# Column strips for the sums over time in a long-convolution filter

## The reference

```python
def hyena_filters(L, w1, b1, w2, b2, w3):
    ...
    h = (h @ w3.astype(f32)).reshape(L, 2, D_A)
    deltas = jnp.abs(jnp.linspace(MIN_DECAY, MAX_DECAY, D_A, dtype=f32))
    h = h * jnp.exp(-t * deltas)[:, None, :]
    h = h / jnp.sum(jnp.abs(h), axis=(0, 1), keepdims=True)
    return h[:, 0], h[:, 1]
```

## Time and profile before

| | us |
|---|---|
| median of three runs | 1622.42 (1619.22 to 1625.27) |
| the profiled execution | 1621.05 |
| its span, first to last instruction | 1619.3 |
| TensorE busy | 1511.1 (93%) |
| DVE busy | 691.1 (43%) |
| ACT busy | 466.4 (29%) |
| POOL busy | 91.9 (6%) |

### The profile page before, as it was taken

One profiled execution on the slowest core, in us unless ns is written; L12 is line 12 of the kernel. 1 busy time (PEld: TensorE's weight loads), 2 busy tenths in 40 slices (PEclk: granted clock), 3 DMA queues, 4 the chain that ended last, 5 costly groups with the idle time before them and its releaser, 6 DMA issues.

```text
span 1619.3 us, 20451 instructions
## 1 busy us (share of the span) xinstructions
PE 1511.1 (93%) x8098; PEld 1230.7 (76%) x8098; DVE 691.1 (43%) x1136; ACT 466.4 (29%) x770; POOL 91.9 (6%) x112
## 2 busy tenths in 40 slices
PE   4788999999899989999899998989999999999897
PEld 1587999999724434388788887878888999999786
DVE  4522223233232352477666776665432222223644
ACT  3332112121121110244444444454541111111321
POOL 2301000000032110100000000000000000000000
PEclk8788999999999999999999999999999999999999
DMA  9310233323300104300000000012220100110611
GB/s 372 141 53 30 79 109 105 120 105 120 141 27 26 62 26 169 118 6 6 20 5 15 5 5 15 0 61 74 79 108 29 40 30 28 35 33 16 231 53 52
DMA packets 29821, 111.16 MB, mean 69 GB/s; under 512 B 3371, under 2 KB 7599, under 8 KB 26064
## 3 DMA queue, kind: packets, MB, share of 16 engines
q1 hardware_dynamic: 28048, 103.46, 17.7%
q10 hardware_dynamic: 1728, 7.08, 1.1%
HBM read 93.86 MB, written 16.66 MB: 68 GB/s over the span
## 4 chain that ended last, share of the span: by engine, by line
PE 85%; DVE 7%; DMA 3%; ACT 2%; issue 2%; SPq 0%; POOL 0%; DVEq 0%; PEld 0%; POOLq 0%; ACTq 0%; PEldq 0%
PE bank L478 58%; PE bank L856 12%; PE bank L778 3%; PE bank L679 3%; PE bank L923 2%; PE bank L771 1%; DMA H<-w_mod_in 1%; PE bank L489 1%; DVE amax L1501 1%; PE bank L628 1%; PE bank L636 1%; DVE SCR L1508 1%; DMA H<-w_oo_in 1%; ACT KV L963 1%; PE bank L501 1%
## 5 line engine op out<-in xcount | busy, mean ns | idle before, releaser
L478 PE MATMUL bank<-H_r,WR_r 128*128 128x384 f32 x1728 | 352.8, 336 | 1.6 <-DVE H_r L1613 1.2
L478 PEld LDWEIGHTS bank<-H_r,WR_r 128*128 128x128 f32 x1728 | 302.6, 188 | 6.3 <-issue 4.2
L478 PE MATMUL bank<-H_r,SCR_r 128*128 128x384 f32 x480 | 161.0, 336 | 0.0
L478 PE MATMUL bank<-SCR 128*128 128x128 f32 x1168 | 141.3, 275 | 2.3 <-DVE H L1514 2.3
L478 PEld LDWEIGHTS bank<-SCR 128*128 128x128 f32 x1168 | 135.7, 192 | 3.2 <-issue 3.2
L478 PE MATMUL bank<-KV,WR 128*128 128x512 f32 (+3 forms) x352 | 126.5, 509 | 1.6 <-ACT KV L1142 1.3
L1181 ACT ACTIVATE SCR<-bank,nmax 128x1152 f32<-128x1152 f32 (+1 forms) x72 | 81.1, 1127 | 148.1 <-DVE nmax L1502 148.1
L478 PEld LDWEIGHTS bank<-KV,WR 128*128 128x128 f32 (+1 forms) x352 | 57.3, 171 | 62.7 <-issue 52.5
L856 PE MATMUL bank<-H_r,WR_r 128*128 128x512 f32 x432 | 99.8, 394 | 3.8 <-DVE SCR L1646 3.8
L478 PE MATMUL bank<-H_r,WX_r 128*128 128x384 f32 x384 | 99.4, 340 | 3.3 <-PEq L571 3.3
L856 PEld LDWEIGHTS bank<-H_r,WR_r 128*128 128x128 f32 x432 | 82.2, 190 | 21.3 <-DVE SCR L1646 4.0
(11 more groups left out here) (249 smaller groups left out, 2194.8 us busy)
## 6 DMA issues: line engine op xcount, KB each, us to landing
H<-w_mod_in SPq DMA_DIRECT2D x6, 2048.0 KB, 16.7
WR<-w_mod_in SPq DMA_DIRECT2D x12, 1024.0 KB, 7.0
SCR<-w_in_in SPq DMA_DIRECT2D x20, 512.0 KB, 3.4
SCR<-x_sample_in SPq DMA_DIRECT2D x16, 512.0 KB, 12.0
WR<-w_io_in SPq DMA_DIRECT2D x16, 512.0 KB, 3.4
sp_rows<-SCR SPq DMA_DIRECT2D x9, 512.0 KB, 2.6
KV<-sp_rows SPq DMA_DIRECT2D x9, 512.0 KB, 8.1
WR<-tf_in SPq DMA_DIRECT2D x4, 1024.0 KB, 4.9
```

Source lines behind the costliest of these rows:

```text
L478: last = nc.tensor.matmul(out, l, r, start=(n == 0), stop=(n == len(pairs) - 1))
```

## The change

The magnitudes of a tile (2 directions x 512 channels) are summed in four strips of 32 columns of the array, each with 32 columns of ones as weights and 256 channels of one direction as columns: strip 0 and 1 the two halves of the forward direction, 2 and 3 those of the backward one. The sums then stand on all 128 partitions (32 equal rows a strip), 256 columns in bank 6 and 256 in bank 7. ACT copies both to all partitions of `norm_rows`. In place of the transposes there are eight products with a selector column, which has a one in the first row of the two strips that belong together, and so adds the directions. POOL makes this selector at the start. The rest is the same.

```diff
-        sel = sb("sel", 2)
+        sel, sel_half = sb("sel", 2), sb("sel_half", 2)
...
-        norm_rows = WX[0:1, 0:2 * DA]
+        norm_rows = WX[:, 0:DA]
...
             def magnitude_sums(t):
                 pe.wait_ge(fh_mag, t + 1)
-                for j in range(2):
-                    last = nc.tensor.matmul(bank[0:1, 6 + t // PROMPT, :], ones[:, 0:1], f_mag[t % 2][:, j, :],
-                                            start=(t in (0, PROMPT) and j == 0), stop=(t >= PROMPT - 1 and j == 1))
+                for g in range(4):
+                    last = nc.tensor.matmul(bank[32 * g:32 * (g + 1), 6 + t // PROMPT, 0:256], ones[:, 0:32], f_mag[t % 2][:, g // 2, g % 2 * 256:(g % 2 + 1) * 256],
+                                            start=t in (0, PROMPT), stop=t >= PROMPT - 1)
                 last.then_inc(nrm_mm, 1)
...
                     for n in range(2 * CA):
-                        last = nc.tensor.transpose(bank[:, 7, n:n + 1], norm_rows[:, n * P:(n + 1) * P], ident[0:1, 0:1])
+                        last = nc.tensor.matmul(bank[:, 7, n:n + 1], norm_rows[:, (n // CA * 2 + n % 2) * P:(n // CA * 2 + n % 2 + 1) * P], sel_half[:, n % CA // 2:n % CA // 2 + 1], start=True, stop=True)
                     last.then_inc(nrm_T, 1)
...
-            nc.scalar.copy(split(norm_rows, 2), bank[0:1, 6:8, :]).then_inc(nrm_cp, 1)
+            nc.scalar.copy(split(norm_rows, 2), bank[:, 6:8, 0:256]).then_inc(nrm_cp, 1)
...
+            link(nc.gpsimd.tensor_tensor(sel_half[:, :], ident[:, 0:64:32], ident[:, 64:P:32], ALU.add))
             link(nc.gpsimd.tensor_tensor(sel[:, :], ident[:, 0:2], ident[:, 32:34], ALU.add))
```

## The result

The changed kernel takes 1631.83 us in the median (1628.24 to 1634.54), the kernel before beside it 1624.62 (1619.22 to 1626.56): a ratio of 1.0048, 95% interval 1.0034 to 1.0062. Forecast were 1616.1 us and faster; it became slower, by 7.8 us of 1624, and lies outside the range. By its number it is rival E, to which the prediction gave 3%, within 1.5 us (1630.5). One slow execution further down, of 5284.1 us among the seven with filter products over all 128 rows, is left out of that run's ratio.

A forecast was written before the change was run, and what follows sets the result against it. TensorE alone was taken to set the filter stage's pace. DVE's product of tile 8 starting 8.7 us earlier, +1.1 for the selector and +1.3 for the tail's clock gave -6.3 us: 1616.1 us from 1622.42, range 1611.5 to 1620.5.

The forecast's parts named there:

- rival E: TensorE's clock falls in the middle of the filter stage: 4.7 us a turn, +8 us, 1630.5 us; chance 0.03.
- The first tile: Start of the filter stage: half clock until 446.9, tile 2's filter ending at 447.85 and not 449.15, 1.3 us saved.
- The strips themselves: Magnitude sums: four strips stream side by side, a tile taking 0.57 us for 1.81 and TensorE's turn 2.48 us.
- tied chain: Filter stage: the path from a tile's filter to its sums takes 2.48 us, equal to TensorE's new turn; nothing added.
- The selector: Behind the first big products: 16 instructions in place of eight transposes, 1.1 us more, bounds 1.0 to 2.1.
- The tail's: End of the filter stage: TensorE's waits lower its clock, one slow stretch costing 1.3 us, bounds 0 and 1.4.
- A: The forecast as summed, with the clock falling once at the end of the filter stage: 1616.1 us; chance 0.46.

The follow-up runs named there:

- first run: The changed kernel with filter products over all 128 rows of the array, the added 64 rows zero: 1616.2 us, ratio 0.9966.

## Why the prediction was wrong

**The step that failed** is in *The first tile*: "until 446.9 half of it is done, and the rest takes 0.95", and the 2.48 us of every turn behind it. It took the end of the slow part, 446.9, as a point in time that stays where it was. It was the work of TensorE that brought it about: the two products (four instructions) of tile 0's old sums over 128 rows, the only work of TensorE between the fall and the return of the clock. The change removed that work, and with it what gave the clock back: in the kernel after the clock stayed at a half through all seven turns, 4.7 us each where 2.48 were forecast. Rival E named the outcome and had its price (+8, measured 7.8), but the wrong reason against it: "the new turn still has 1.72 us of full-width filter in 2.48". The filter is full in columns and half in height; its rows say 64*128. That E's +8 came out is in part luck: it counts seven turns of +1.0, where six were measured and nothing lost ahead of them, and it leaves out the 1.7 us of slow big products.

**The question was put wrongly.** E asked whether the clock falls in the middle of the stage. In the three profiles in which the light stream began a turn at full clock it held it: the two with products ahead of tile 0, and the one with full height for three tiles. In the kernel after the clock had fallen before the first turn, and then the question is what wins it back. Where it falls is no fixed point either. Of the six profiles with 64 rows in the filter products of tiles 0 and 1, five lose the clock within these products, at 436.5 to 437.1, and only the kernel before's loses it in the wait behind them, at 443.5; of the seven with 128 rows none loses it before 441.8. So half height in front of the wait goes with an earlier fall; why the kernel before's execution was spared is open.

**The strips themselves** cost what was summed: 0.57 us a tile at full clock and a turn of 2.48 us (first run). DVE, POOL, ACT and the tied chain added nothing. The first filter product to the first big product took 31.8 us in that run against 40.1, so 8.3 us less where 8.7 were forecast. The Trainium skill ("TensorE: Matmul & The Clock Gate", "Measured speedup vs the span model") has 3.07 times for four row strips. The sums here went from 1.81 to 0.57 us, 3.2 times with the switch in it: near that figure as a whole, while the 0.13 us a tile that the prediction worked out from it isn't seen.

**The selector** took 1.1 us more, as summed (482.98 to 484.96 in the first run, 0.88 before). **The tail's** slow stretch came, as taken in A, and cost 1.7 us (15.67 for 13.97), over the bound of 1.4 (1.4 to 2.3 in the six profiles of strips at full clock without products in the tail's waits); it was costed by the sums, whose slow stretch was not all at half clock. -8.3 + 1.1 + 1.7 is -5.5 us, and the first run measured 0.9966, which is -5.5. So the sum was right to 0.8 us for a kernel whose clock comes back, closer than the interval of that run (2.8 us either way) can show, and 14 us off for this one. The ends of the range don't follow from the bounds named, which give some 1612.7 and 1620.0 and not 1611.5 and 1620.5; the measured time lies above either.

**Where a rule and the trace differ.** The Trainium skill says in "TensorE: Matmul & The Clock Gate", section "What's actually happening", that a monitor sets the clock "based on how busy the PE has been recently". By the profile's busy time the trace doesn't agree: TensorE was busy for 23.60 of 23.60 us at 1.2 GHz, and without the sums for 24.42 of 24.42. With the same filter products over 128 rows, or 0.84 us of added 128-row products a tile, the clock came back.

## What to carry to other kernels

Before TensorE work is taken out of a stage that follows a wait, look at what gives the clock back behind that wait, and whether the work that stays has the array's full height; the busy share of a stretch doesn't show it, its granted clock and the products' rows (64*128 or 128*128) do. Zero rows of the streamed operand that bring a half-height product to full height cost no time (ratio 0.9998 on the kernel before) and were worth some 13 us here (0.9966 against 1.0048). Short waits count as well: behind two of 2 us, with 0.6 us of strips between, the next big products lost 1.7 us, which products without use in the waits saved.

## What was not expected of the hardware

The same instruction stream on TensorE has two courses, depending on the clock with which it begins: 4.7 us a turn through all seven turns in the kernel after, 2.48 us a turn in the two profiled executions that entered it at full clock. And more work can be faster: 0.84 us a tile of products whose result nobody uses made the changed kernel 5.5 us quicker.
